# Sample rows' state products in row groups over stacked heads, gate quarters moved, and a re-cut last group in a one-core decoder step

## What is computed

```python
# mLSTM, per chunk (a sample's 4 tokens are one chunk)
C_new = decay[..., None, None] * C + jnp.einsum('bshd,bshv->bhdv', kw, vc)
n_new = decay[..., None] * n + jnp.sum(kw, axis=1)
...
# gated delta rule
Sm = gl_c[..., None, None] * Sm + jnp.einsum('bhld,bhlv->bhdv', kd_c, v_new)
...
mixed = (jax.nn.sigmoid(gate_a) * (h_a @ w_br_mlstm) + jax.nn.sigmoid(gate_b) * (h_b @ w_br_gdn)
         + jax.nn.sigmoid(gate_c) * (h_c @ w_br_xattn))
x = x + mixed @ w_out
x = x + hier_moe(rmsnorm(x, norm_ffn), ...)     # top-1 of 4 groups, top-2 of its 4 experts
...
y_prompt = rmsnorm(xp, final_norm)
y_sample = rmsnorm(xs, final_norm)
```

## Time and profile before

| | |
|---|---|
| runs of the kernel before, us | 789.66, 788.73, 789.96 (median 789.66) |
| the profiled execution, us | 789.25 |
| its span in the trace, us | 787.2 |
| PE, DVE, ACT, POOL busy, us | 733.2, 280.0, 165.1, 61.9 |
| DMA moved | 187.25 MB, mean 238 GB/s |

### The profile page before, as it was taken

The page is one execution under the profiler, slowest core; times in us unless marked ns, Lnnn a source line. Parts: engine busy times, 40 slices in busy tenths (PEclk is TensorE's granted clock), DMA queues, the critical chain, the costliest instruction groups (busy, mean ns, idle before and its releaser), DMA issues.

```text
span 787.2 us, 10576 instructions
## 1 busy us (share of the span) xinstructions
PE 733.2 (93%) x4379; PEld 429.2 (55%) x4379; DVE 280.0 (36%) x725; ACT 165.1 (21%) x377; POOL 61.9 (8%) x93
## 2 busy tenths in 40 slices
PE   6999999999998999999999999999999778988795
PEld 3544558877755877777777764653334323333221
DVE  1241022575784661473264162251223100110244
ACT  3221221321265311321232100331010100000014
POOL 3010200010230000000010001021000000001010
PEclk9999999999999999999999999999999989999898
DMA  9983700871697502032325537866999999999991
GB/s 266 323 291 107 200 16 2 279 260 37 198 383 259 162 2 107 1 125 91 107 75 208 204 124 257 357 273 249 358 428 429 406 427 430 411 426 401 428 348 63
DMA packets 49327, 187.25 MB, mean 238 GB/s; under 512 B 5224, under 2 KB 5469, under 8 KB 45178
## 3 DMA queue, kind: packets, MB, share of 16 engines
q1 hardware_dynamic: 39888, 155.52, 51.3%
q0 software_dynamic: 9280, 30.96, 12.0%
q10 hardware_dynamic: 106, 0.03, 0.0%
HBM read 174.43 MB, written 16.83 MB: 243 GB/s over the span
## 4 chain that ended last, share of the span: by engine, by line
PE 79%; DMA 13%; DVE 3%; ACT 2%; issue 1%; SPq 1%; ACTq 0%; DVEq 0%
PE PS L658 13%; PE PS L1008 12%; DMA arena<-in_w_exp_down 9%; PE PS L1402 8%; PE PS L1020 6%; PE PS L747 6%; PE PS L1432 6%; DMA ring<-in_w_exp_down 3%; PE PS L669 2%; PE PS L774 2%; PE PS L644 2%; PE PS L1306 1%; PE PS L733 1%; SPq L1507 1%; PE PS L1388 1%
## 5 line engine op out<-in xcount | busy, mean ns | idle before, releaser
L1402 PE MATMUL PS<-ring,arena 128*64 128x512 f32 x416 | 98.4, 629 | 11.3 <-issue 11.2
L1008 PE MATMUL PS<-hT,ring 128*128 128x288 f32 x384 | 101.9, 414 | 0.0
L1733 ACT ACTIVATE arena<-PS 128x512 f32<-128x512 f32 (+7 forms) x128 | 50.9, 421 | 194.1 <-PE PS L1008 62.6
L1008 PEld LDWEIGHTS PS<-hT,ring 128*128 128x128 f32 x384 | 70.3, 190 | 19.0 <-issue 0.9
L1402 PEld LDWEIGHTS PS<-ring,arena 128*64 128x64 f32 x416 | 34.4, 145 | 70.7 <-issue 70.7
L658 PE MATMUL PS<-ring,hT 128*128 128x512 f32 x160 | 70.3, 596 | 0.0
L1733 ACT ACTIVATE brT<-PS 128x256 f32<-128x256 f32 (+4 forms) x37 | 15.6, 424 | 202.3 <-PE PS L1402 150.9
L1020 PE MATMUL PS<-brT,ring 128*128 128x288 f32 x192 | 51.3, 414 | 0.3 <-DVE arena L2526 0.3
L658 PEld LDWEIGHTS PS<-ring,hT 128*128 128x128 f32 x160 | 30.0, 190 | 37.2 <-issue 37.2
L747 PE MATMUL PS<-hT,ring 128*128 128x288 f32 x192 | 49.3, 411 | 0.8 <-DVE small L2295 0.8
L2929 DVE SCALAR_TENSOR_TENSOR brT<-brT,PS 128x256 f32<-128x256 f32 x16 | 6.7, 421 | 111.2 <-ACT brT L1733 111.2
(11 more groups left out here) (388 smaller groups left out, 893.7 us busy)
## 6 DMA issues: line engine op xcount, KB each, us to landing
ring<-in_w_in SPq DMA_DIRECT2D x15, 2048.0 KB, 11.7
ring<-in_w_exp_gate SPq DMA_DIRECT2D x13, 2048.0 KB, 23.6
ring<-in_w_exp_up SPq DMA_DIRECT2D x13, 2048.0 KB, 27.9
ring<-in_w_exp_down SPq DMA_DIRECT2D x8, 2048.0 KB, 26.2
arena<-in_w_exp_down SPq DMA_DIRECT2D x6, 2048.0 KB, 29.5
arena<-in_w_exp_gate SPq DMA_DIRECT2D x3, 2048.0 KB, 17.7
arena<-in_w_exp_up SPq DMA_DIRECT2D x3, 2048.0 KB, 22.5
moe_in<-in_table SPq DMA_DIRECT2D x2, 2048.0 KB, 21.5
```

Of the source, the lines that this page charges most:

```text
L1008: ins = pe.matmul(PS[:, b, 0:T], w[:, 512 * k + 128 * (c % 4):512 * k + 128 * (c % 4) + 128], hT[:, k, :], start=(k == 0), stop=(k == KD - 1))
L1402: ins = pe.matmul(o[64 * hf:64 * hf + 64, :], hg[:, k, 64 * e:64 * e + 64], w[:, :, 512 * k + 256 * hf:512 * k + 256 * hf + 256], start=(k ...
L1733: return act.activation(o, i, f, **kw)
```

## The change

The constants' table repeats the samples' mask `C_BCOL` over four groups of 32 partitions. For mLSTM, DVE writes each head's weighted keys and values of the samples to its own 32 partitions of `k_stack` and `v_stack` (eight instructions in place of one), and one instruction builds `vblk` for all heads on 128 partitions in place of four. PE goes through three batches of samples (3, 3, 2), and in each through the four heads: head `h` reads partitions 32h to 32h+31 and writes bank 1, 2, 3 or 5. The queries stand behind the first batch, `fill(10)` and `turn_keys(0)` behind the second, `fill(11)` and `turn_keys(1)` behind the third. DVE copies the norms' column and marks the heads behind all batches. The gated delta rule's products are made alike: ACT makes one more copy (`vn_stack`), `kds` and `vnb` are stacked, and `states_out(g)` runs over four samples and all heads; the first stands ahead of the "hb" quarters, the second ahead of the branch loop, and DVE marks the heads in the second. `PART_AT[0]` gets a point "caches" ahead of `read_caches` with three quarters, and "raw" has one instead of two. In the last group the sample rows leave `to_tokens` for `to_samples`: four calls of 256 columns in four column groups, one bank per pair; `stay_busy(3)` adds three 128x512 calls, whose result nobody reads, ahead of `down(0)`. At the end ACT no longer scales the samples' first half, DVE scales their whole row, and the second prompt tile is written out in two halves.

```diff
@@ PE, mLSTM
-                for h in range(H):
-                    pe.wait_ge(sg("vblk"), h + 1)
-                    for g, (b0, b1) in enumerate(((0, 3), (3, 6), (6, 8))):
-                        bk = (1, 2, 3)[g]
+                pe.wait_ge(sg("vblk"), 1)
+                for g, (b0, b1) in enumerate(STATE_BATCHES):
+                    for h in range(H):
+                        bk = (1, 2, 3, 5)[h]
                         o = use(("Cs", h, g), bk)
-                        pe.matmul(o[:, 0:(b1 - b0) * DA], k_t[0:n, t, 128 * h:128 * h + 128],
-                                  vblk[h % 2][:, b0:b1, :].rearrange("p b v -> p (b v)"),
+                        pe.matmul(o[:, 0:(b1 - b0) * DA], k_stack[NS * h:NS * h + NS, :],
+                                  vblk[NS * h:NS * h + NS, b0:b1, :].rearrange("p b v -> p (b v)"),
                                   start=True, stop=True).then_inc(full[bk], 1)
-                    if h == 0:
+                    if g == 0:
                         query(2)
                         query(3)
...
+                    else:
+                        fill(9 + g)
+                        turn_keys(g - 1)
@@ PE, gated delta rule
-        def states_out(h):
-
-            pe.wait_ge(sg("vnb"), h + 1)
-            for g in range(2):
-                o = use(("So2", h, g), g)
...
+        def states_out(g):
+
+            pe.wait_ge(sg("vnb"), 1)
+            for h in range(H):
+                b = (0, 2, 3, 4)[h]
+                o = use(("So2", h, g), b)
+                pe.matmul(o, kds[NS * h:NS * h + NS, :],
+                          vnb[NS * h:NS * h + NS, 4 * g:4 * g + 4, :].rearrange("p b v -> p (b v)"),
+                          start=True, stop=True).then_inc(full[b], 1)
...
         turn_raw(0)
+        part_at(0, "caches")
         read_caches()
...
-        states_out(0)
+        states_out(1)
         pe.wait_ge(*taken(("hbT", 2)))
         for c in range(KD):
             branch(1, c, (7, 5, 6)[c % 3])
-            if c in STATE_AT:
-                states_out(STATE_AT[c])
@@ PE, last group
             turn_act(1, p, g)
+            if BUSY:
+                stay_busy(BUSY, p)
             down(0, p, g)
             gate_up(2, p, g)
+            to_samples(0, p)
             to_tokens(0, 0, p)
...
+        def to_samples(pr_, p):
+
+            pe.wait_ge(*lmoved("pT", pr_, p))
+            for nn in range(2):
+                pe.wait_ge(*moved("dn", 2 * pr_ + nn, p, G - 1))
+            pe.wait_ge(*ltaken("ys", pr_, p))
+            for c in range(4):
+                ins = pe.matmul(lbank("ys", pr_)[NS * c:NS * c + NS, 0:256], turned_w[pr_][:, SEQ:T],
+                                outp[pr_][:, 256 * c:256 * c + 256], start=True, stop=True)
+            ins.then_inc(lfull("ys", pr_), 1)
+
+        def stay_busy(n, p):
+
+            pe.wait_ge(*gtaken("dn", 0, p, G - 1))
+            for _ in range(n):
+                pe.matmul(gbank("dn", 0), ident, cst[:, 0:512], start=True, stop=True)
@@ DVE, mLSTM
-                masked_values(0)
-                masked_values(1)
+                dve.wait_ge(sg("kw"), 3)
+                tt(vblk, bc(v_stack.unsqueeze(1), 128, NB, DA),
+                   bc(cst[:, C_BCOL:C_BCOL + NB].unsqueeze(2), 128, NB, DA), ALU.mult).then_inc(sg("vblk"), 1)
...
+                for h in range(H):
+                    dve.wait_ge(*taken(("Cs", h, 2)))
+                    cp(nst[:, h:NB * H:H], Cs[:, h, :, DH]).then_inc(sg("Cs"), 1)
```

184 lines of the change are left out of this document (96 added, 88 removed).

## The result

| | before | changed |
|---|---|---|
| median of the first runs, us | 789.81 (788.73 to 790.23, 4 runs) | 775.99 (773.82 to 776.76, 4 runs) |
| ratio | | 0.9819 (0.9805 to 0.9834) |
| profiled execution, us | 789.25 | 773.82 |
| span of it, us | 787.2 | 771.7 |

The change makes the kernel 1.8% faster, 14 us. The forecast was 777.6 us, 773 to 783. Ten more runs of the changed kernel, made beside the experiments, reach from 774.22 to 780.0; the median of all 14 is 775.3. The kernel before, run beside them, had medians of 789.74 to 790.04.

What follows compares the result with a forecast made beforehand. PE was taken to bound the kernel up to about 541 us, then full DMA engines in a rigid stage. 789.25 - 3.65 - 3.87 - 4.8 + 0.3 = 777.2, plus 0.4 for the median: 777.6 us, range 773 to 783.

Steps and rivals of the forecast that it cites:

- term 1: mLSTM state products (`Cs`): batches over four row groups cost 3.4 us for 7.7, less a 0.65 us stall: -3.65 us.
- term 2: Three gate quarters ahead of `read_caches` fill PE's wait and keep the clock up: -3.87 us (bounds -1.9 to -4.4).
- term 3: Gated-delta state products (`So2`): two batches of four calls, 2.85 us for 7.65: -4.8 us (bounds 0 and -5.7).
- term 4: Last group: slow `gate_up(2)` +1.7, token calls -0.85, ACT output moved to DVE -0.55; sum +0.3 us.
- rival (a): Last group: `gate_up(2)` stays at full clock, 1.7 us less, 775.9 us; chance 0.2.
- The stall for bank 5: Last `Cs` batch: fourth head's call waits until ACT empties bank 5 after `turn_keys(0)`; 0.65 us lost.
- rival (d): `Cs` outputs: block of `C_s` writes lands late, `silu(0)` and PE wait; at 14.5 us landing 780.6 us; chance 0.14.
- Rival (b): `Cs` and `So2` batches: row-group overlap nearly free, gains of 1.0 and 0.9 us more, 775.7 us; chance 0.13.
- the +1.7 for a slow `gate_up(2)`: Last group: slow block moves from `down(0)`, hidden by DMA, to `gate_up(2)` on the path: +1.7 us (0 to +2.4).
- Rigid from the fifth pair on: Saturated expert stage begins earlier by what PE gains before 541 us, about 12.3 us, and is no shorter.
- rival (c): `Cs` and `So2` batches: row groups don't overlap, both gains are 0, 785.9 us; chance 0.1.
- (e): `Cs` and `So2` batches: concurrent writes to the same partitions make batches slower than calls in a row; 801 at double price; chance 0.03.

Runs made afterwards that it cites:

- e7: Changed kernel with `C_s` written by sample, `turn_keys(0)` ahead of `fill(10)`, no `stay_busy`, `to_samples(0)` and `to_tokens(0, 0)` ahead of `gate_up(2)`; median 778.72 us.
- e4: Changed kernel with the first three gate quarters put back behind `read_caches`; median 778.44 us.
- e2: Changed kernel with `C_s` written sample by sample behind each batch, eight writes of 256 KB in place of four of 512 KB; median 775.13 us.
- e5: Changed kernel with the `Cs` products run head by head again in banks 1 to 3, stacked operands kept; median 777.9 us.
- e6: Changed kernel with `So2` run head by head again in two banks, ahead of and between the branches; median 780.16 us.
- e8: Changed kernel with `C_s` written by sample and the fourth head's last `Cs` batch in bank 0; median 774.64 us.

## Why the forecast came out as it did

The time, 775.99, lies 1.6 us under the forecast. Against the forecast, and by the single edits, term 1 brought 1.0 us less, term 2 0.4 less, term 3 1.3 more and term 4 1.2 more (by the pair of profiles). That is 3.9 us of misses, of which 1.1 us remain when they are added with their signs: that they nearly cancel is luck, and rival (a)'s 775.9 is met by luck too: its condition, `gate_up(2)` at full clock, came true, but the terms beside it moved. By its steps:

- **Term 1, -3.65.** Measured -4.25 up to `scores(0)`. The forecast took four times 0.14 us for the weight loads of a batch; the row of `scores` from which that came has its 0.14 once. A batch of 387 columns costs 0.72 + 0.14 = 0.86 and not 1.2, one of 512 columns 0.95 + 0.12. The stall for bank 5 was seen (0.65 taken), and came to 1.1 us (1.75 for a batch of 0.64, as e7 has it). Then +1.58 for the block of writes, to which the forecast gave a chance of 0.14 as rival (d). Its place and its waiters were right. Its threshold of 11.5 us was too low: the last write was issued at 208.26 and not 210.7 and wanted at 221.3, so it decided from 13.1. The landing time in the forecast itself was wrong, because the bound came from writes issued one by one (at most 9.1 us) and these were issued as a block (15.5 us). Net -2.67. Rival (b) was right on the price of a batch (0.6 more in term 1 after the longer stall, 0.7 in term 3), rival (d) on what stands against it (1.58), and they nearly cancel.
- **Term 2, -3.87.** Right in mechanism: -3.46 when undone alone. The filled wait and the clock at 1.00 are as put, and 3.63 us for the calls (3.8) and 0.40 us of waiting for `hcs` (0.5) lie near it. The size was off by 0.4: up to the `kT2` transposes, counted from the last `scores`, e4 takes 1.51 us more and the kernel before 1.70, where 1.93 was put.
- **Term 3, -4.8.** Measured -6.09. The batches cost 2.15 and not 2.85 (the same wrong step as in term 1; the 0.85 taken for a call of 512 columns was low, a call in the pairs of the earlier trace rows takes 0.95), and the 0.6 us for cutting the branches in pieces was not in the sum at all.
- **Term 4, +0.3.** -0.89 in the profile pair, -1.0 in the two distances that repeat when undone alone. The end and the token calls were nearly right (-1.0 for -1.4). The step that failed is the +1.7 for a slow `gate_up(2)`, from "waits of 1.99 us and more in this stage were followed by a slow block". It was read from one execution. In six profiles `gate_up(2)` stands behind a wait of 2.53 to 2.56 us; in one of them it is slow (8.56 us, e2, and there the last stage takes 253.56 us, 1.6 more), in five it runs in 7.09. At two other places, with waits of 2.62 to 2.84 us, a slow block did follow every time. Why the places differ stays open.
- **Rigid from the fifth pair on.** Right. The first `gate_up` came 14.6 us earlier, `down(0)` 14.5 us, the end 15.5 us; and what e4, e5 and e6 took away ahead of it (4.0, 2.8 and 6.6 us against the changed kernel's first profile) came back at the end nearly whole (4.4, 2.5 and 6.4).
- **Not in the sum:** the 1.69 us of column six, `keep_busy(3)`, which had the low clock in the profile of before (4.54 us for 6 instructions) and full clock in that of after (2.84), and 0.53 us ahead of all edits. This is 2.2 us of the 15.43 between the two profiles that are no effect of the change.

By the sentences from the Trainium skill ("TensorE: Matmul & The Clock Gate", Part 3), 3.07 times for four row tiles of 512 columns, the sum was 776.5. Measured here, four calls against four in a row, it is 3.5 times with 512 columns (1.07 for four times 0.95), so the measurement decides. It is 3.3 with 387 (0.86 for four times 0.72) and about 3.0 with 258 (0.64 for four times 0.48, e7's batch of the last samples).

The rival (c), no overlap, and (e), a disturbance of writes to the same partitions, are out: the batches run at little more than one call's price (1.07 us for 0.95), in four banks of the same 128 partitions.

## What to carry to other kernels

Price small calls in different row groups at one call plus 0.12 to 0.16 us, as measured here for three sizes, and look next at what their results now do all at once: outputs that used to leave one by one leave as a block, and whoever waits for the last of them waits for the block. Before a bank is used earlier, ask who holds it now as well as who takes it next. A low clock behind a wait, read in one profile, is not yet a rule: at one place it came in 14 of 14 profiles, at another in one of six. Put it in the range, take a second profile, and compare profiles by distances between fixed marks, in which such blocks show up as steps.

## What was not expected of the hardware

- Four row groups of 32 rows that write the same 128 PSUM partitions in four banks: 1.07 us for four calls of 512 columns, against 0.95 for one.
- The same wait of 2.55 us at the same place is followed by 7.09 us or by 8.56 us for the same 32 instructions, from one profile to the next; the projection at 493 us slows to 8.81 without any idle time ahead of it in three profiles of fourteen.
- Cutting 64 instructions on 128 rows in four pieces, with pairs of 32-row calls between them, made them 0.61 us longer without idle time (16.24 against 15.63 us).
- A write of 512 KB landed after 3.9 to 15.5 us when four were issued within 5 us, and after 3.8 to 9.7 us when they were issued one by one (e5); eight of 256 KB, issued from 192 to 207 us, landed after 2.7 to 4.3 us (e2; in e8 one took 8.2).
